# Retention layer: value, gate and output products as pairs of 64 rows on the two row halves of TensorE

## What is computed

```python
def retention_mixer(h, pos, w_in, w_out):
    q, k, v, z = _split(h @ w_in, ODD_SPLITS)          # 4 heads, q and k 256 wide, v and z 512 wide
    q, k = xpos_rotate(q, pos), xpos_rotate(k, pos) * (RET_QK_DIM ** -0.5)
    o = rms_norm(multiscale_retention(q, k, v))
    return (silu(z) * o) @ w_out                       # added to the residual stream
```

## Time and profile before

| | |
|---|---|
| median of 3 runs | 1672.25 us (1671.3 to 1672.84) |
| the profiled execution | 1674.15 us, of which the span is 1672.1 us |
| TensorE busy in the span | 1640.6 us (98%) |
| VectorE, ScalarE, GpSimd busy | 679.7 us (41%), 411.9 us (25%), 226.1 us (14%) |
| odd layer on TensorE | from about 776 us to 1190 us |
| mean HBM traffic | 275 GB/s over the span |

### The profile page before, as it was taken

One profiled execution on the slowest core, in us unless ns is written; L12 is line 12 of the kernel. 1 busy time (PEld: TensorE's weight loads), 2 busy tenths in 40 slices (PEclk: granted clock), 3 DMA queues, 4 the chain that ended last, 5 costly groups with the idle time before them and its releaser, 6 DMA issues.

```text
span 1672.1 us, 22392 instructions
## 1 busy us (share of the span) xinstructions
PE 1640.6 (98%) x9377; PEld 1055.1 (63%) x9377; DVE 679.7 (41%) x1238; ACT 411.9 (25%) x766; POOL 226.1 (14%) x162
## 2 busy tenths in 40 slices
PE   7999899999999999999999999999999999999997
PEld 7878788745445454547888888888754544445443
DVE  4887763533423243334413223242623333324333
ACT  4576663300000000004332414223500000000000
POOL 1600101000000000003444344432100000000000
PEclk9999999999999999999999999999999999999999
DMA  9420222899999999997313122223699999999995
GB/s 207 106 51 1 66 90 101 345 420 425 423 427 427 425 427 423 426 424 271 105 51 101 65 87 101 92 82 143 265 389 424 427 423 427 426 425 425 426 426 230
DMA packets 79383, 460.86 MB, mean 276 GB/s; under 512 B 6960, under 2 KB 32784, under 8 KB 53552
## 3 DMA queue, kind: packets, MB, share of 16 engines
q1 hardware_dynamic: 78544, 457.03, 67.5%
q0 software_dynamic: 736, 2.34, 1.2%
HBM read 457.25 MB, written 2.10 MB: 275 GB/s over the span
## 4 chain that ended last, share of the span: by engine, by line
PE 93%; DVE 2%; DMA 2%; ACT 2%; issue 1%; SPq 0%; DVEq 0%; ACTq 0%
PE bank L161 31%; PE bank L1958 26%; PE bank L1978 13%; PE bank L1985 7%; PE bank L1916 7%; DMA ring<-in_w_up_dram 1%; PE bank L1969 1%; PE bank L1622 1%; DMA ring<-in_w_in_even_dram 0%; PE bank L1909 0%; PE bank L2542 0%; PE bank L2655 0%; PE bank L1610 0%; PE bank L1032 0%; PE bank L1941 0%
## 5 line engine op out<-in xcount | busy, mean ns | idle before, releaser
L1958 PE MATMUL bank<-ring,SCR 128*64 128x512 f32 x1760 | 445.9, 592 | 1.5 <-issue 1.0
L161 PE MATMUL bank<-ring_r 128*128 128x512 f32 (+2 forms) x1120 | 337.5, 380 | 1.5 <-DVE ring_r L445 1.5
L1958 PEld LDWEIGHTS bank<-ring,SCR 128*64 128x64 f32 x1760 | 146.3, 137 | 245.5 <-issue 245.0
L161 PEld LDWEIGHTS bank<-ring_r 128*128 128x128 f32 x1120 | 206.1, 188 | 41.2 <-issue 2.9
L1978 PE MATMUL bank<-ring,SCR 128*64 128x512 f32 x880 | 226.7, 595 | 0.0
L1950 DVE SCALAR_TENSOR_TENSOR X<-bank,AU,X 128x512 f32<-128x512 f32 x256 | 173.7, 744 | 88.9 <-PE bank L1985 88.9
L1997 DVE TENSOR_TENSOR SCR<-SCR,bank 128x512 f32<-128x512 f32 x32 | 22.0, 688 | 361.8 <-PE bank L1958 361.8
L1978 PEld LDWEIGHTS bank<-ring,SCR 128*64 128x64 f32 x880 | 70.1, 137 | 121.3 <-issue 121.3
L161 PE MATMUL bank<-ring_r,SCR_r 128*128 128x512 f32 x576 | 138.5, 395 | 0.0
L2511 POOL TENSOR_TENSOR ring_r<-ring,ring_r 128x1024 fp32r<-128x1024 f32 x48 | 117.0, 2470 | 143.9 <-ACT ring_r L2497 143.9
L1985 PE MATMUL bank<-SCR_r 128*128 128x512 f32 x512 | 131.9, 400 | 0.3 <-DVE SCR_r L1994 0.3
(11 more groups left out here) (463 smaller groups left out, 1884.3 us busy)
## 6 DMA issues: line engine op xcount, KB each, us to landing
ring<-in_w_gate_dram SPq DMA_DIRECT2D x53, 2048.0 KB, 16.5
ring<-in_w_down_dram SPq DMA_DIRECT2D x51, 2048.0 KB, 15.9
ring<-in_w_up_dram SPq DMA_DIRECT2D x50, 2048.0 KB, 19.6
ring<-in_w_in_odd_dram SPq DMA_DIRECT2D x8, 2048.0 KB, 9.2
SCR<-in_w_up_dram SPq DMA_DIRECT2D x10, 1024.0 KB, 15.5
SCR<-in_w_gate_dram SPq DMA_DIRECT2D x9, 1024.0 KB, 12.3
SCR<-in_w_down_dram SPq DMA_DIRECT2D x9, 1024.0 KB, 18.3
ring<-in_w_in_even_dram SPq DMA_DIRECT2D x16, 512.0 KB, 6.5
```

What stands on the lines that cost most here:

```text
L161: mm = pe.matmul(out, lhs[a], rhs[b], start=(first and i == 0), stop=(last and i == 2))
L1958: mm = pe.matmul(bank[SLOTS * u:SLOTS * u + SLOTS, :], xt[:, k, SLOTS * u:SLOTS * u + SLOTS], w[u](k), start=(k == 0), stop=(k == KT - 1))
```

## The change

1. A new helper, `split_rows_mm`, makes each of the three matmuls as two: rows 0 to 63 of the contraction into one bank, rows 64 to 127 into a second. It is used for V of heads 1 to 3, for Z(1) to Z(3) of heads 0 to 2, and for all output products of heads 0 to 2: 288 + 216 + 288 = 792 matmuls of 128 rows become 792 pairs of 64 rows.
2. The bank pairs are 6 and 7, and 4 and 5, in turn. VectorE sums the two banks: for V a copy into the home of the lower part and an addition (`v_sum`), for Z the same into the home of the gate (`z_sum`), for the output products two residual additions in place of one. ScalarE and `v_lower` then read SBUF.
3. `v_sum(h, t + 1)` stands ahead of `v_lower(h, t)` in VectorE's stream. TensorE's wait of V(2) and V(3) for `r_vl` is as before.
4. All four transposes now stand within the query and key products (2 and 3 ahead of the last of the four), since the output products need banks 6 and 7; n = 0 waits for all four lower parts.
5. The quarter loads of expert weights 7 and 8 are gone: they are loaded whole, after the first gate product.

```diff
+        def split_rows_mm(pe, outs, lhs, rhs, first, last):
+
+            for i, (a, b) in enumerate(((0, 0), (0, 1), (1, 0))):
+                for r, out in enumerate(outs):
+                    rows = slice(64 * r, 64 * r + 64)
+                    mm = pe.matmul(out, lhs[a][rows], rhs[b][rows], start=(first and i == 0), stop=(last and i == 2))
+            return mm
...
-            for a in range(4):
-                sp.wait_ge(*((sg("first_gate"), 3 * l + a + 1) if a < 3 else mw("gate", 1)))
-                for n in IN_QUARTERS:
-                    load_quarter(n, a)
-            for n in range(E_SLOTS + 2, tail):
+            for n in range(E_SLOTS, tail):
                 load(n)
...
                 for par in range(2):
+                    for t in (2, 3) if s + par == 2 and between else ():
+                        ret_yt_pe(pe, h - 1, t)
...
+                        if h:
+                            mm = split_rows_mm(pe, [b[:, :] for b in out_rows(t)], [a[:, k, t * P:(t + 1) * P] for a in (HTU, HT_r)], [a[:, k, :] for a in w], k == 0, k == KT - 1)
+                            continue
...
                         pe.wait_ge(sg("r_al"), 6 * h + 2)
+                    if kt == 1 and h:
+                        pe.wait_ge(sg("r_vl"), NT * h + 3)
...
                     for n in range(8):
-                        if n == 2:
-                            ret_yt_pe(pe, h, 2)
-                            ret_yt_pe(pe, h, 3)
-                        ret_out_pe(pe, h, n)
+                        ret_out_rows_pe(pe, h, n)
...
+        def out_rows(n):
+
+            return PB[6 - 2 * (n % 2)], PB[7 - 2 * (n % 2)]
+
+        def ret_out_rows_pe(pe, h, n):
...
+            if n == 0:
+                pe.wait_ge(sg("r_ytl"), NT * h + NT)
...
+            def v_sum(h, t):
+                if h:
+                    dve.wait_ge(sg("r_v"), NT * h + t + 1)
+                    a, b = out_rows(t)
+                    step.then(dve.tensor_copy(VL32[:, t, :], a[:, :]))
+                    dve.tensor_tensor(VL32[:, t, :], VL32[:, t, :], b[:, :], ALU.add).then_inc(sg("r_sum"), 1)
...
+                    if t < NT - 1:
+                        v_sum(h, t + 1)
                     v_lower(h, t)
...
+                    if h < RH - 1:
+                        step.then(dve.tensor_tensor(xs, xs, out_rows(n)[0][:, :], ALU.add))
+                        dve.tensor_tensor(xs, xs, out_rows(n)[1][:, :], ALU.add).then_inc(resid, 1)
```

More of the change, by code:

```diff
@@ L255, in expert_landings @@
         def expert_landings(l, s, n):
-            return sum(4 if m in IN_QUARTERS else len(weight_pieces(s)) for m in range(n) if home(l, m) == s)
+            return len(weight_pieces(s)) * sum(home(l, m) == s for m in range(n))
         def landed(c):
@@ L1950, in add_gated, with hidden_mm @@
             return dve.scalar_tensor_tensor(x_part(m), bank[:, :], GN[b][:, m // 2:m // 2 + 1], x_part(m), ALU.mult, ALU.add)
-        def hidden_mm(pe, bank, us, w, xt, ready=(), read={}):
+        def hidden_mm(pe, bank, us, w, xt, ready=()):
             for k in range(KT):
@@ L2048, in gate @@
                     ready = [(0, mw("xt_out", 2 * i + 4 if duo_after(i) else NE))]
-                quarters = {k: sg("first_gate") for k in (1, 3, 5)} if is_at(i, 0) else {}
-                hidden_mm(pe, BG, range(2), w_two(l, 0, i, KT), x_of(n), ready, quarters).then_inc(ms("gate"), 1)
+                hidden_mm(pe, BG, range(2), w_two(l, 0, i, KT), x_of(n), ready).then_inc(ms("gate"), 1)
             def up(i, n):
@@ L2633, in ret_pe, with z_in_rows, sums @@
                     router_pe(pe, 1, 8)
+        def z_in_rows(h, t):
+            return t > 0 and h < RH - 1
+        def sums(h, z):
+            return (NT * h - NT if h else 0) + 3 * h + ((NT if h else 0) if z else 0)
         def ret_z_pe(pe, h, t):
@@ L2637, in ret_z_pe @@
             w = [a.rearrange("p (k n) -> p k n", k=KT) for a in w]
-            if t < 2:
+            if t == 0 and h:
+                pe.wait_ge(sg("r_vl"), NT * h + NT)
+            elif t == 1 and z_in_rows(h, t):
+                pe.wait_ge(sg("r_at"), NT * (h + 1))
+            elif t < 2:
                 pe.wait_ge(sg("r_vl"), NT * h + t + 3)
@@ L2651, in ret_yt_pe @@
                 pe.wait_ge(sg("r_at"), NT * (h + 1))
+                if h < RH - 1:
+                    pe.wait_ge(sg("r_sum"), sums(h, True) + 3)
             else:
@@ L2674, in ret_out_pe @@
             mm.then_inc(sg("r_out"), 1)
+        def out_rows(n):
+            return PB[6 - 2 * (n % 2)], PB[7 - 2 * (n % 2)]
+        def ret_out_rows_pe(pe, h, n):
+            i, c, w = odd_chunk("out", h)
+            w = [a.rearrange("p (k n) -> p k n", k=4) for a in w]
+            t, half = n // 2, n % 2
+            if n == 0:
+                pe.wait_ge(sg("r_ytl"), NT * h + NT)
+            elif n == 1:
+                pe.wait_ge(sg("r_zs"), NT * h + NT)
+            else:
+                pe.wait_ge(resid, R_MOE0 + 8 * h + n - 1)
+            for j in range(4):
+                if n == 0:
+                    pe.wait_ge(sg("r_lower"), 4 * i + j + 1)
+                mm = split_rows_mm(pe, [b[:, :] for b in out_rows(n)], [a[:, t, j, :] for a in (YTr, YTl)],
+                                   [a[:, j, half * 512:(half + 1) * 512] for a in w], j == 0, j == 3)
+            mm.then_inc(sg("r_out"), 1)
         def ret_act(act, step):
@@ L2682, in z_out @@
             def z_out(h, t):
+                if z_in_rows(h, t):
+                    act.wait_ge(sg("r_sum"), sums(h, True) + t)
+                    act.activation(ZS[:, t, :], ZS[:, t, :], ACT.Silu, scale=rstd[:, t:t + 1]).then_inc(sg("r_zs"), 1)
+                    return
                 act.wait_ge(sg("r_z"), NT * h + t + 1)
@@ L2772, in ret_dve @@
             for h in range(RH):
+                v_sum(h, 0)
                 for t in range(NT) if h else range(2, NT):
@@ L2792, in ret_dve @@
                     rotate(h + 1, both[0:1])
-                for t in range(2) if h < RH - 1 else range(1, 3):
+                for t in range(NT) if h < RH - 1 else range(1, 3):
                     yt_lower(h, t)
@@ L2802, in ret_dve @@
                     dve.wait_ge(resid, R_MOE0 + 8 * h)
[L2803 removed]
+                    if h < RH - 1:
+                        step.then(dve.tensor_tensor(xs, xs, out_rows(n)[0][:, :], ALU.add))
+                        dve.tensor_tensor(xs, xs, out_rows(n)[1][:, :], ALU.add).then_inc(resid, 1)
+                    else:
+                        dve.tensor_tensor(xs, xs, PB[4 + n % 2][:, :], ALU.add).then_inc(resid, 1)
                     if h == RH - 1:
```

33 lines of the change are left out of this document (21 added, 12 removed).

## The result

The changed kernel took 1735.39 us (median of 4 runs, 1734.53 to 1736.72); the kernel before took 1672.01 us beside it. The ratio is 1.038, with a 95% interval of 1.0362 to 1.0398: 63 us slower. The forecast was 1715, with 1698 to 1734 as the range, so the direction and the place were right and the size was not.

What follows compares the result with a forecast made beforehand. TensorE, busy 98% of the span, was taken as the bound. Terms -9.1 + 2.3 + 18.2 + 26.4 + 5 = +42.8 us on 1674.15 gave 1717.0, less 1.9 for the median: 1715 us, range 1698 to 1734.

Steps and rivals of the forecast that it cites:

- 1. row pairs: All 792 row pairs: each starts 0.216 us apart against 0.2275 for a whole matmul, 9.1 us saved.
- 2. changes of mode: TensorE switching between whole and halved array: 12 switches at 0.19 us each, +2.3 us.
- 3. first output product: First output product waits for all four lower parts behind ScalarE's cast: 6.07 us idle in three heads, +18.2 us.
- 4. V(2), V(3), scores: TensorE waits for VectorE: 2.5 us at V(2) and V(3), 3.8 before the scores, heads 1 to 3, +26.4 us.
- 5. the other sums: Z sums and second residual additions lie beside TensorE's work: 0, at most 1.5 us at each of 33 places.
- 6. clock: Half clock around the odd layer's stalls: 0.8 us per long stall, 0.9 per V stage, +5 us, bounds 0 and 15.
- 7. expert loads: Expert weight loads issued 5 us later, absorbed by idle DMA time: 0, between -1 and +3 us.
- The fear that GpSimd would slow the lower parts of V: Value stage: lower parts meeting GpSimd's weight splitting would raise the stalls from 8.8 to 12 us a head.
- most of it would be the change of weights, which two halves hide from each other: Row pairs: claimed source of most of the 0.0115 us a whole matmul costs above a pair.
- the pairs gain nothing: Rival, 15%: row pairs save no time, by the page's rule or for float32r; 1724 us.
- the clock that falls at nearly every stall: Rival, 16%: clock falls at nearly every stall, or GpSimd slows lower parts; +10 to +20, 1725 to 1735 us.

Runs made afterwards that it cites:

- the filled one: Changed kernel with matmuls whose results are not used put just before the waits of V(2), V(3), the scores and the first output product: 1718.84 us.
- the kernel without quarters: Kernel before the change with the quarter loads of expert weights alone taken out: 1673.51 us, ratio 1.0004.
- run with the scores' wait alone: Changed kernel, V(2) and V(3) waiting for sums, value-weight cast behind all four copies, keys' lower part still behind V(3)'s sum and V(2)'s lower part: 1692.04 us.

## Why the prediction was right or wrong

| term | predicted | measured | by |
|---|---|---|---|
| 1. row pairs | -9.1 | 0 | 48 pairs 11.18 us, 48 whole matmuls 11.17 |
| 2. changes of mode | +2.3 | +3.0 | 12 x 0.25 |
| 3. first output product | +18.2 | +18.0 | 3 x (5.83 + 0.16) |
| 4. V(2), V(3), scores | +26.4 | +24.7 | 6 x (2.17 + 0.16), 3 x (3.40 + 0.16) |
| 5. the other sums | 0 | at most +1 | no wait before Z or output products 1 to 7 |
| 6. clock | +5 | +17.1 | changed kernel less the filled one; 1.5 of it away from any stall |
| 7. expert loads | 0 | 0 | the ratio of the kernel without quarters |

The measured terms add up to 63.8 us, and the odd layer grew by 63.5.

**Right: the stalls.** Their number, places and releasers were as worked out from the listings and the durations of the kernel before. The three long ones were off by 0.1 us each, those of part 4 by 0.2 each: the last hand-over before an output or value product took 0.04 us where 0.15 was taken, the lower parts of V 0.66 to 0.68 where 0.75 was, and that of the keys 1.15 where 1.23 was. The fear that GpSimd would slow the lower parts of V was not put to the test: GpSimd had ended at 923.93, before the first of them began at 924.58, and ran again only at 956.97, behind the scores; the other two heads are alike.

**Wrong: the step "most of it would be the change of weights, which two halves hide from each other" (part 1).** The 0.216 was real, but it came from float32 records and was set against float32r matmuls: the types differed as well as the halving. Pairs in float32r keep the same step as whole matmuls: 0 gained where 9.1 was forecast. The triples of the changed kernel start 0.68 us apart (844.83 to 845.51), 0.227 a pair:

```profile
844.83 0.39 PE L169 MATMUL bank<-ring_r,HT_r 64*128 64x512 f32 x2
845.05 0.62 PE L169 MATMUL bank<-ring_r 64*128 64x512 f32 x4
845.51 0.39 PE L169 MATMUL bank<-ring_r,HT_r 64*128 64x512 f32 x2
```

A control stood in the trace of the kernel before: float32 products on the whole array with a weight load for each record, in its chain of waits,

```profile
158.81 3.57 PE bank L936 x32
```

0.1116 us for two passes of 128 columns (0.1067 at 2.4 GHz). A change of weights of the whole array costs 5 ns there at most, so it was no ground for the 11.5 ns a matmul that the pairs were to save. The rival "the pairs gain nothing", with 15%, was what happened. The Trainium skill (TensorEngine Tiling (Array Packing), "Performance Considerations"), which recommends row tiling for contractions of up to 64 rows, was right here, and the measurement agrees with it.

**Wrong in size: the clock (part 6).** The mechanism held and the cost was 17.1 us where I took 5; my upper bound of 15 was too low as well. At 0.50 a pair starts 0.427 us after the one before, where it was 0.227 at 1.00:

```profile
933.88 0.64 PE L169 MATMUL bank<-ring_r,HT_r 64*128 64x512 f32 x2
934.31 1.06 PE L169 MATMUL bank<-ring_r 64*128 64x512 f32 x4
```

So a microsecond of half clock that is full of matmuls costs about 0.47. With TensorE's busy time in the fourteen stretches this gives an estimate of where the cost lay:

| | taken | half clock us | with matmuls | estimate us |
|---|---|---|---|---|
| three long stalls | 2.4 | 20.5 | 12.4 | 5.8 |
| three value stages | 2.7 | 23.9 | 22.7 | 10.6 |
| end of the layer | 0 | 3.4 | 3.4 | 1.5 (5.38 less 3.89) |

The estimates add up to 17.9, a little above the 17.1. For a long stall I took one stretch of 3.4 us, in part inside the stall: the clock stayed low for 6.8 us each time, of which 3.6 to 4.85 held matmuls, 1.9 us a stall where I took 0.8. The larger error is the value stages. I took 0.9 us for each, as if one stretch touched it: there were two, two and three, and hardly any of it fell into a stall, 3.5 us a head. The run with the scores' wait alone shows that even an isolated stall of 3.4 us costs 1.4 more by the clock. The Trainium skill (TensorE: Matmul & The Clock Gate, Part 1) says that idling brings the array back to half rate; the trace agrees with 0.50 at every long stall.

The terms add up to 21 us more than the forecast sum: 9.8 by parts 1 and 2, 12.1 by part 6 and 1.0 by part 5, less 1.9 by which parts 3 and 4 were too high. Two of the rivals came true together, the pairs without gain (15%) and the clock that falls at nearly every stall (16%); the range took in either, but not both.

## What to carry to other kernels

Compare a candidate price only with rows that differ in one thing. Before believing that a tiling mode hides a cost, find the same cost in the same data type without the mode. When sums or copies are put between a product and its consumer, walk each in-order stream for what now stands ahead of the instruction that frees a bank: a wait for the lower part where the sum would do, and a cast ahead of two copies, cost some 58 of the 63 us here, clock included. A stall of TensorE costs more than its length: with the clock it was about 7.9 us for 6.0 (by the estimate above), and 5.0 for 3.6.

## What was not expected of the hardware

- A float32r matmul of 512 columns starts 0.2267 us after the one before, 13 ns above the streaming time at 2.4 GHz, and two on the row halves do so together. Float32 passes of 512 columns take 0.2145 to 0.2147 us on column halves and on the whole array alike. At half clock the float32r pairs and whole matmuls start 0.427 us apart, which is the streaming time of 512 columns at 1.2 GHz with nothing above it; the 13 ns show at full clock alone. Why float32r has them was not settled, and no run here shows whether column halves in float32r would.
- A change between whole and halved array cost 0.25 us each way, where the one place read before gave 0.19.
- The half clock lasted 6.8 us at each of the stalls of 5.8 us, and 3.4 us near a lone stall of 3.4 us. One stall of 2.2 us, behind at least 8.6 us of matmuls without a break, was followed by 3.4 us of it; two others like it were not.
